# Shift sums of the first adaLN modulation by TensorE, smaller first loads in a new order, squares ahead of the silu row

## The reference, cut to what matters

```
c_act = silu(c)                                      # (1, 1024)
mods = split(c_act @ ada_w[i] + ada_b[i], 9)         # sh1, sc1, g1, ..., 1024 numbers each
h = x * rsqrt(mean(x * x) + 1e-6) * norm_g * (1 + sc1) + sh1
x = x + 0.5 * g1 * swiglu_ffn(h, w_in, w_out)
```

## Time and profile before

| | us |
|---|---|
| median of 3 runs | 2138.91 (2138.76 to 2140.07) |
| profiled execution, its own time | 2136.69 |
| span of its trace | 2134.4 |
| TensorE busy in the span | 2080.9 (97%) |
| VectorE, ScalarE, GpSimd busy | 1160.6, 605.3, 56.1 |
| first matmul starts | 19.07 |
| last matmul of the prologue starts | 60.00 |

### The profile page before, as it was taken

The page is one execution under the profiler, slowest core; times in us unless marked ns, Lnnn a source line. Parts: engine busy times, 40 slices in busy tenths (PEclk is TensorE's granted clock), DMA queues, the critical chain, the costliest instruction groups (busy, mean ns, idle before and its releaser), DMA issues.

```text
span 2134.4 us, 26594 instructions
## 1 busy us (share of the span) xinstructions
PE 2080.9 (97%) x10614; PEld 1763.3 (83%) x10614; DVE 1160.6 (54%) x1669; ACT 605.3 (28%) x709; POOL 56.1 (3%) x60
## 2 busy tenths in 40 slices
PE   4999999999999999999999999999999999999998
PEld 3788888999898889888888977778878798888886
DVE  7677545645545436886445665643458554333322
ACT  2222222323323224222222333332331233222222
POOL 2000000000000000000000000000003000000000
PEclk9999999999999999999999999999998999999999
DMA  8556565523223243666554254444677223323231
GB/s 314 159 177 206 167 200 175 170 73 123 82 81 104 69 146 130 199 228 232 172 172 157 82 157 136 145 131 162 218 243 276 83 72 113 102 81 101 94 106 55
DMA packets 245377, 314.46 MB, mean 147 GB/s; under 512 B 31777, under 2 KB 218401, under 8 KB 242993
## 3 DMA queue, kind: packets, MB, share of 16 engines
q1 hardware_dynamic: 204672, 282.67, 40.2%
q10 hardware_dynamic: 40624, 30.68, 4.6%
HBM read 289.99 MB, written 27.53 MB: 149 GB/s over the span
## 4 chain that ended last, share of the span: by engine, by line
PE 74%; issue 18%; DVE 5%; DMA 1%; ACT 1%; POOL 0%; SPq 0%; ACTq 0%; POOLq 0%; DVEq 0%
PE ps L1712 18%; PE ps L1714 18%; PE ps L1713 18%; PE ps L1739 6%; PE ps L1740 6%; PE ps L1743 6%; PE ps L1992 1%; DVE ada_first L925 1%; DVE tur L1285 1%; DMA y_dram<-s_buf 1%; DVE rot L1285 0%; DMA csil<-in_c 0%; PE ps L1994 0%; DVE w_lo L915 0%; PE ps L2108 0%
## 5 line engine op out<-in xcount | busy, mean ns | idle before, releaser
L522 ACT ACTIVATE w_hi<-w_raw 128x1024 fp32r<-128x1024 f32 x352 | 345.9, 1029 | 343.9 <-PE ps L1714 247.9
L915 DVE TENSOR_TENSOR w_lo<-w_raw,w_hi 128x1024 fp32r<-128x1024 f32 x174 | 212.7, 1222 | 391.3 <-ACT w_hi L522 389.8
L1712 PE MATMUL ps<-g_hi,w_lo 128*128 128x512 f32 (+1 forms) x952 | 346.1, 364 | 0.0
L1714 PE MATMUL ps<-g_hi,w_hi 128*128 128x512 f32 (+1 forms) x952 | 345.3, 363 | 0.0
L1713 PE MATMUL ps<-g_lo,w_hi 128*128 128x512 f32 (+1 forms) x952 | 345.3, 363 | 0.0
L1712 PE MATMUL ps<-h_hi,w_lo 128*128 128x512 f32 x880 | 344.7, 392 | 0.0
L1714 PE MATMUL ps<-h_hi,w_hi 128*128 128x512 f32 x880 | 343.0, 390 | 0.0
L1713 PE MATMUL ps<-h_lo,w_hi 128*128 128x512 f32 x880 | 343.0, 390 | 0.0
L1739 PE MATMUL ps<-h_hi,w_lo 128*128 128x512 f32 x688 | 269.3, 391 | 2.0 <-DVE w_lo L915 2.0
L1740 PE MATMUL ps<-h_hi,w_hi 128*128 128x512 f32 x688 | 268.4, 390 | 0.0
L1743 PE MATMUL ps<-h_lo,w_hi 128*128 128x512 f32 x688 | 212.2, 390 | 0.0
(11 more groups left out here) (261 smaller groups left out, 2457.6 us busy)
## 6 DMA issues: line engine op xcount, KB each, us to landing
w_raw<-in_ffn_w_in SPq DMA_DIRECT2D x86, 1024.0 KB, 7.0
ada_raw<-in_ada_w SPq DMA_DIRECT2D x128, 512.0 KB, 4.6
w_raw<-in_ffn_w_out SPq DMA_DIRECT2D x32, 1024.0 KB, 5.5
w_raw<-in_ret_w_in SPq DMA_DIRECT2D x24, 1024.0 KB, 5.2
w_raw<-in_ffn_w_out SPq DMA_DIRECT2D x16, 768.0 KB, 4.4
tb<-s_rec SPq DMA_DIRECT2D x6, 2048.0 KB, 9.1
w_raw<-in_ret_w_out SPq DMA_DIRECT2D x8, 1024.0 KB, 5.4
w_raw<-in_s_w_glu SPq DMA_DIRECT2D x8, 1024.0 KB, 5.8
```

Source lines behind the costliest of these rows:

```text
L522: copy = lambda o, i: nc.scalar.activation(o, i, ACT.Copy)
L915: V.tensor_tensor(w_lo[k % 2][:, 0:HALF, :], w_raw[k % 2][:, 0:HALF, :], raw_f32(w_hi[k % 2][:, 0:HALF, :]), ALU.subtract).then_inc(w_lo_h ...
L1712: nc.tensor.matmul(o, wl, xh, start=start, stop=False)
L1714: return nc.tensor.matmul(o, wh, xh, start=False, stop=stop)
```

## The change

SP and ACT no longer load shift and scale weights of a tile as one piece. `ada_shift[t]` (4 KB in each partition) now holds untransposed weights, `ada_scale[t]` transposed ones, and they come in a new order. PE computes the shift of a tile: eight accumulating f32 matmuls of one column, with a 128x128 block of `ada_shift` as the stationary operand and a column of silu(c) (`c_col`, 128x8, a small load and a small ACT instruction of its own) as the moving one. DVE adds the bias in three instructions (two tiles, two tiles, four tiles) instead of eight modulations. ACT squares x before it takes the silu of the row. POOL takes one power at the start whose result is not used. Names: `tb_in` becomes `piece_in`, which also counts the pieces of `ada_shift`.

```diff
+            sp.dma_start(c_col[:], ins["c_col"]).then_inc(par_in, 16)
...
-            sp.dma_start(ada_first[:, 0], ins["ada_first"][0]).then_inc(tile_in[0], 16)
-            for h in range(2):
+            shift_piece(0)
+            shift_piece(1)
+            first_chunk(0)
+            shift_piece(2)
+            shift_piece(3)
+            first_chunk(1)
+            scale_piece(1)
+            for t in range(HALF, KT):
+                shift_piece(t)
+                scale_piece(t - 2)
+            scale_piece(KT - 2)
+            scale_piece(KT - 1)
...
+            nc.gpsimd.tensor_tensor(rstd[:, 0:1], ones[:], mhalf[:, 0:1], ALU.pow).then_inc(consts_e, 1)
...
-            act.wait_ge(c_row_in, 16)
-            nc.scalar.activation(csil[:], csil[:], ACT.Silu).then_inc(csil_done, 1)
+            act.wait_ge(par_in, 32)
+            nc.scalar.activation(c_col[:], c_col[:], ACT.Silu).then_inc(csil_done, 1)
             for pr in range(OUT_PAIRS):
                 act.wait_ge(x_in[pr], 16)
                 nc.scalar.activation(squares[:, 2 * pr:2 * pr + 2], ...)
+            act.wait_ge(c_row_in, 16)
+            nc.scalar.activation(csil[:], csil[:], ACT.Silu).then_inc(csil_done, 1)
...
-                act.wait_ge(mods_ready, t + 1)
+                act.wait_ge(mods_ready, 1 + (t > 1) + (t > 3))
...
+                def first_shifts(i, bank, at):
+                    dve.wait_ge(shift_sums, i + 1)
+                    V.tensor_tensor(mods[:, at], ps[:, bank, at], par[:, at], ALU.add).then_inc(mods_ready, 1)
...
                     norm_mult(t)
+                    if t == HALF:
+                        first_shifts(2, 4, slice(HALF, KT))
                     if t + 1 < KT:
-                        first_shift(t + 1)
+                        first_scale(t + 1)
                     norm_lo(0, t, 0)
+                    if t == 0:
+                        first_shifts(1, 7, slice(2, HALF))
                     if t in (1, 2):
                         split_first(t - 1, 1)
-                    if t + 1 < KT:
-                        first_scale(t + 1)
...
+            def first_shift(t, bank):
+                pe.wait_ge(piece_in[t], 16)
+                for r in range(KT):
+                    m = nc.tensor.matmul(ps[:, bank, t:t + 1], ada_shift[:, t, r], c_col[:, r:r + 1],
+                                         start=r == 0, stop=r == KT - 1)
+                return m
+
             def begin():
+                pe.wait_ge(csil_done, 1)
+                first_shift(0, 6)
+                first_shift(1, 6).then_inc(shift_sums, 1)
                 sum_squares(0)
+                first_shift(2, 7)
                 spread_roots(0)
+                first_shift(3, 7).then_inc(shift_sums, 1)
                 pe.wait_ge(w_lo_half, 3)
                 for t in range(KT):
+                    if t in (1, 2):
+                        first_shift(t + 3, 4)
+                    if t == 3:
+                        first_shift(6, 4)
+                        first_shift(7, 4).then_inc(shift_sums, 1)
```

More of the change, by code:

```diff
@@ L152, in build @@
         squares = sb("squares", [P, KT, L], F32, g_at)
-        ada_first = sb("ada_first", [P, KT, 2, D], F32, g_at + HB)
+        ada_shift = sb("ada_shift", [P, KT, KT, P], F32, g_at + HB)
+        ada_scale = sb("ada_scale", [P, KT, D], F32, g_at + 3 * HB)
+        c_col = sb("c_col", [P, KT], F32, g_at + 5 * HB + 6144)
         sm = sb("sm", [P, len(SMALL), G], F32, g_at + 5 * HB)
@@ L260, in build @@
             sem("ys_done"), sem("ys_stored"), sem("lag_done"), sem("lag_copied"), sem("lag_stored"))
-        tb_in = [sem(f"tb_in{b}") for b in range(KT)]
+        piece_in = [sem(f"piece_in{b}") for b in range(KT)]
+        shift_sums = sem("shift_sums")
         u_out = [sem(f"u_out{r}") for r in range(2)]
@@ L398, in table @@
                 def table(b):
-                    sp.dma_start(tables[b][:], rec[b]).then_inc(tb_in[b], 16)
+                    sp.dma_start(tables[b][:], rec[b]).then_inc(piece_in[b], 16)
                 glu_pair(0)
@@ L421, in _, with shift_piece, scale_piece, first_chunk @@
             sp.dma_start(csil[:], ins["c"].broadcast_to([P, D])).then_inc(c_row_in, 16)
-            sp.dma_start(ada_first[:, 0], ins["ada_first"][0]).then_inc(tile_in[0], 16)
-            for h in range(2):
+            def shift_piece(t):
+                sp.dma_start(ada_shift[:, t], ins["ada_shift"][t]).then_inc(piece_in[t], 16)
+            def scale_piece(t):
+                sp.dma_start(ada_scale[:, t], ins["ada_scale"][t]).then_inc(tile_in[t], 16)
+            def first_chunk(h):
                 r = slice(h * HALF, (h + 1) * HALF)
                 sp.dma_start(w_raw[0][:, r], ffn_in[0][:, r, 0:CW]).then_inc(w_first[0][h], 16)
-            for t in range(2, KT):
-                sp.dma_start(ada_first[:, t], ins["ada_first"][t]).then_inc(tile_in[t], 16)
+            shift_piece(0)
[10 more added lines that the diff above has]
+            scale_piece(KT - 1)
             sp.dma_start(sm[:, 0:2], ins["s5_a"]).then_inc(params_in, 16)
@@ L1148, in split_first, with first_scale @@
                                     ALU.subtract).then_inc((w_lo_half, w_lo_done)[h], 1)
-                def first_shift(t):
+                def first_shifts(i, bank, at):
+                    dve.wait_ge(shift_sums, i + 1)
+                    V.tensor_tensor(mods[:, at], ps[:, bank, at], par[:, at], ALU.add).then_inc(mods_ready, 1)
+                def first_scale(t):
                     dve.wait_ge(tile_in[t], 16)
-                    modulation(ada_first[:, t, 0], slice(t, t + 1)).then_inc(mods_ready, 1)
-                def first_scale(t):
                     at = slice(KT + t, KT + t + 1)
-                    st(modulation(ada_first[:, t, 1], at))
+                    st(modulation(ada_scale[:, t], at))
                     st.wait()
@@ L1160, in first_scale @@
                     st.wait()
-                dve.wait_ge(par_in, 16)
-                dve.wait_ge(csil_done, 1)
-                first_shift(0)
+                dve.wait_ge(par_in, 32)
+                dve.wait_ge(csil_done, 2)
                 dve.wait_ge(stat_done, 1)
                 V.tensor_scalar(ms[:], ps[:, 4, 0:TT], 1.0 / D, NORM_EPS, ALU.mult, ALU.add).then_inc(ms_done, 1)
+                st(V.memset(acc[:], 0.0))
                 first_scale(0)
-                st(V.memset(acc[:], 0.0))
+                first_shifts(0, 6, slice(0, 2))
                 for k in range(2):
@@ L2089, in states @@
                         pe.wait_ge(us_pool, b - US_DVE + 1)
-                    pe.wait_ge(tb_in[b], 16)
+                    pe.wait_ge(piece_in[b], 32)
                     if b >= 2:
@@ L2242, in lay_out @@
     r["x_t"] = a["x"][0][:, PERM].T.reshape(KT, P, L).transpose(1, 0, 2)
-    r["ada_w"] = wide(a["ada_w"], N_MOD, 2).transpose(0, 2, 1).reshape(2, N_MOD * KT, P, D)
-    r["ada_first"] = r["ada_w"][0, :2 * KT].reshape(2, KT, P, D).transpose(1, 2, 0, 3)
+    ada = wide(a["ada_w"], N_MOD, 2)
+    r["ada_w"] = ada.transpose(0, 2, 1).reshape(2, N_MOD * KT, P, D)
+    r["ada_shift"] = ada[0, :, :D].reshape(KT, P, KT, P).transpose(2, 1, 0, 3)
+    r["ada_scale"] = r["ada_w"][0, KT:2 * KT]
+    r["c_col"] = a["c"].reshape(KT, P).T
     r["par"] = np.concatenate([t.reshape(-1, P) for t in (
```

12 lines of the change are left out of this document (6 added, 6 removed).

## The result

The changed kernel is slower: 2141.36 us against 2137.70 (medians of 20 runs each), a ratio of 1.0017 with a 95% interval of 1.0010 to 1.0023, 3.7 us. The profiled execution of the change took 2144.03, the longest of the 20, with a span of 2142.2. The profiled execution of before took 2136.69, a little less than its median, so the two traces lie 7.3 us apart and the medians 3.7.

What follows compares the result with a forecast made beforehand. PE was taken to bound the changed prologue, its gapless matmuls ending 1.3 us later; added to the median 2138.91 this gave 2140.2 us, own range 2138.5 to 2142.5 (60%), wider range 2133.8 to 2143.8.

Steps and rivals of the forecast that it cites:

- What bounds: Prologue: DVE bounds the loop over tiles before the change; afterwards PE runs without a gap and ends 1.3 us later.
- The price of a record: One-column shift matmuls on PE: records 0.213 us apart ahead of tile 0, 0.114 behind it; 16 records per shift.
- Rival 1: Ahead of tile 0: any busy matmul raises the clock by the middle of the first shifts; 2133.9 us, chance 11%.
- The start of TensorE: Prologue: PE's first matmul at about 12.8 us, when piece 0 lands, between bounds of 11.2 and 14.3.
- The fall of the clock behind pieces 6 and 7: Ahead of tile 3: 3.7 us without wide matmuls could lower the clock, costing 1.7 us and leading to 2141.9.
- The sum: PE's prologue: tile 0 at 30.1, plus 22.0 wide matmuls, 2.0 lower clock, 7.7 pieces; last wide start at 61.6.
- Rival 2: Piece 4, between tiles 0 and 1: the clock is still down, costing 4.0 us beyond the forecast; 2144.2, chance 15%.
- The wait in tile 4: DVE in tile 4 idles 6.6 us, from 41.5 to 48.1, until PE finishes piece 7.
- The early root: POOL's first root after the sums of squares: the early power saves 1.0 us (1.99 to 1.01), no gain in time.
- The first h_hi: ACT's h_hi of tile 0 comes at 26.5, behind two weight copies, before PE asks at 30.1.
- rival 3: Loop over tiles: shifts nearly free on PE, DVE bounds; loop ends 9.2 us earlier, 2129.7, chance 5%.
- The same, slower or faster: Whole kernel, limit 0.2%: chance 0.69 the same, 0.16 slower, 0.15 faster.

Runs made afterwards that it cites:

- e3: The changed kernel with only 1 of 8 matmuls of each shift, waits, loads and order kept; ratio to before 0.9956.
- e4: The changed kernel with unused 512-column f32 matmuls, 8 ahead of the first shift and 5 behind the sums of squares; ratio to before 1.0023.
- e8: The kernel before, all shifts on VectorE, with the change's load pieces and order but without the small column load; ratio to before 0.9998.
- e2: The changed kernel with 4 of 8 matmuls of each shift, waits, loads and order kept; ratio to before 0.9983.
- e5: The changed kernel with shift 7 moved from ahead of tile 3 to ahead of tile 4, with its own bias addition; ratio to before 1.0005.
- e7: The changed kernel, shift 7 ahead of tile 4, unused wide f32 matmuls: five before shift 0, one each behind shift 0, sums, roots; ratio to before 1.0003.
- e1: The kernel before with one part of the change alone: ACT squares x ahead of the silu of row c; ratio to before 0.9988.

## Why the prediction was right

- **What bounds.** Right. VectorE bounded the prologue before, TensorE does now. With an eighth of the shift matmuls (e3) the gain of VectorE's shorter loop comes out. The work of TensorE ahead of tile 0 came out by its rows, forecast first and measured in brackets: pieces 0 and 1 6.8 us (6.8), sums 1.7 (1.7), piece 2 3.4 (3.4), roots 1.9 (1.85), piece 3 3.4 (3.3).
- **The price of a record.** Right ahead of tile 0, 0.213 us, and a little high behind it: 0.114 forecast, from a group of 8, and 0.106 to 0.109 measured in groups of 16 and 32 (a piece with its change of width 1.8, not 1.93). Weighing the stretch at 1598 us over the rule of the Trainium skill, page "TensorE: Matmul & The Clock Gate", section on the HAM clock gate (activity releases the throttle), was the decision. This trace does not bear the rule out for one-column matmuls: 80 records from 14.25 to 31.3, 72 of one column and the 8 of the roots, left the clock down, and e4 shows it rise with wide ones. Rival 1 fell with that.
- **The start of TensorE.** Mis-sized. 12.8 was forecast, 14.25 measured, within the stated bounds of 11.2 to 14.3. The forecast left out that the new load of the column moves every later issue of SP: piece 0 was issued at 3.16, where the old first piece was at 2.61 (and piece 0 of e8, without that load, at 2.61). It took 11.0 to land:

```profile
3.16 1.44 SPq L428 DMA_DIRECT2D ada_shift<-in_ada_shift x2
```

```profile
ada_shift<-in_ada_shift SPq DMA_DIRECT2D x1, 512.0 KB, 11.0
```

  The wait's releaser in the first row of TensorE, ACT's csil, is not its cause. TensorE's first wait is for piece 0 and for the silu of the column, done at 6.0 us, and not for that of the row, done at 14.1; in e2 the same wait is put down to the transfer. In other executions piece 0 came at 13.4 to 14.0.
- **The fall of the clock behind pieces 6 and 7.** Priced at 1.7 us with no chance of its own, left out of the sum, and it came. The stretch at 1608 to 1622 was held against it and misled: there 64 columns kept the clock up, here one column did not. The pieces themselves still ran at the upper level; the fall hit eight wide records of tile 3 and cost 1.5 us.
- **The sum.** The last wide start was forecast at 61.6 and came at 64.58 (the second record of the row at 64.35). The 3.0 us are 1.45 of a later start and 1.5 of the fall, and 0.5 for tile 0, of which all twelve wide matmuls and not ten ran at the lower level; against these, the pieces came out some 0.5 cheaper. These are the terms that were mis-sized; the path, TensorE without a gap, was the forecast one.
- **How much of the hit is luck.** The forecast was 1.3 us later, the medians say 3.7, outside the "1 to 3 us later". The median of 2141.36 still lies near the forecast 2140.2, and inside its own range (2138.5 to 2142.5), because the 3 runs of before that it started from had a median of 2138.91 and the 20 runs have 2137.70.
- **Rival 2.** It came close. Its condition, a rise of the clock more than 5.1 us after the first wide matmul, was met: piece 4 started 5.27 us behind it with the clock still down. But the clock rose within the piece, which took 1.97 us and not 3.41, so the rival's 4.0 us were not paid. In e5, whose program is the same up to there, the rise came 3.1 us behind the first wide matmul, so that this term too differs from one execution to the next.
- **The wait in tile 4.** Right: 6.6 us forecast, 6.51 measured, released by TensorE, and without cost in itself.
- **The early root.** Its gain of 1.0 us was wrong (2.34, not 1.01), and that cost nothing, as TensorE was busy with piece 2.
- **The first h_hi.** The working has three values for the earliest h_hi of tile 0 (26.5, 25.9 for rival 1, 25.4 for rival 3). In e3, where it decides, tile 0 starts at 26.11. The forecast does not hang on it.
- **The same, slower or faster.** 0.17% is within the 0.2% set as the limit; with 20 runs it is told apart from no change.
- **Rival 3**, the loop bound by VectorE, was priced about rightly: 9.2 us, and e3, with an eighth of the records, gains 9.7 at the prologue's end.

## What to carry to other kernels

Before work is moved to an engine that looks idle, count its records there by the price that the trace shows for that very shape at that very place: a one-column f32 matmul here is two records and costs about as much as a wide one of the split weights, which is one record (0.21 and 0.23 us at the full clock, 0.43 for both at the lower), and 64 of them outweighed seven modulations of 1.2 us. TensorE's idle time in front of its first wide work was worth only half of what the rows later in the kernel suggest, since the clock was at its lower level there, and 17 us of matmuls, nearly all of one column, left it so. When a change has several parts, time them apart: here the one that only moved a statement is 2.6 us faster by itself, and the whole is 3.7 us slower.

## What the runs showed of the hardware that was not expected

- TensorE busy without a gap with one-column f32 matmuls let its clock fall from the upper to the lower level: in e4 at about 21.2, behind 40 such records from 16.69 on, and in the change at about 50.7, behind 32 records and five wide ones. With 64 columns, from 1608 to 1622, it stayed up.
- In e7 the clock stayed low for 20.5 us, from 17.4 to 37.9, in which TensorE was busy all the time, with some wide matmuls among the narrow.
- ScalarE loaded its table a second time in e1, where Square came ahead of Silu (1.28 us at 12.17), and only once up to there where a Silu came first, as in the change (at 4.40).
- The time of an execution outside the span of its trace was 1.79 to 1.92 us with an early power on GpSimd and 2.22 to 2.35 without, in every execution; the cause is open.
